# Third mixer's compact inverse: the stream step between the two products of a level moved behind the second product

## The reference

```
h   = rms_norm(x)
z   = h @ w_in                       # columns for four mixers, and four sets of merge gates
o_i = mixer_i(z_i), i = 1..4         # HGRN2, RWKV-7, GLA, mLSTM; 4 heads each
mix = sum_i (o_i @ w_branch_i) * sigmoid(z_gate_i)
x   = x + mix @ w_out
x   = x + relu(rms_norm(x) @ w_up)^2 @ w_down
y   = rms_norm(x)
```

## Time and profile before

| | us |
|---|---|
| median of 3 runs | 2150.78 |
| lowest, highest | 2146.99, 2151.19 |
| the profiled execution, its own time | 2154.51 |
| its span | 2152.6 |
| PE busy | 2074.8 |
| PEld busy | 1961.0 |
| DVE busy | 1032.9 |
| ACT busy | 607.4 |
| POOL busy | 455.1 |
| first L1336 of tile 0, last L1345 of tile 7 start at | 865.0, 1091.7 |

### The profile page before, as it was taken

How to read it: one execution, slowest core, us unless ns; L and a number is a source line. 1 busy time by engine, 2 the same in 40 slices (tenths; PEclk the granted TensorE clock), 3 DMA queues, 4 the chain that set the end, 5 groups by cost and what they waited for, 6 DMA issues and landing times.

```text
span 2152.6 us, 37101 instructions
## 1 busy us (share of the span) xinstructions
PE 2074.8 (96%) x15253; PEld 1961.0 (91%) x15253; DVE 1032.9 (48%) x1611; ACT 607.4 (28%) x821; POOL 455.1 (21%) x463
## 2 busy tenths in 40 slices
PE   6999999999999989999899999999999999999997
PEld 4998888999999879788789999999999999999996
DVE  4052334365755536444443785522222236556666
ACT  4432224332322154222222430101101023333343
POOL 1122113344554421100002671200000010000020
PEclk9999999999999999999999999999999999999999
DMA  4123225322122242111023652311112242111112
GB/s 170 41 60 85 60 81 153 101 70 65 56 72 66 84 141 85 48 42 42 23 61 142 241 190 80 128 39 49 49 39 69 79 186 90 43 49 39 49 40 100
DMA packets 50852, 177.96 MB, mean 83 GB/s; under 512 B 6481, under 2 KB 10033, under 8 KB 50497
## 3 DMA queue, kind: packets, MB, share of 16 engines
q1 hardware_dynamic: 25296, 85.77, 13.7%
q0 software_dynamic: 17648, 61.31, 8.4%
q10 hardware_dynamic: 7808, 29.41, 3.5%
HBM read 128.95 MB, written 47.51 MB: 82 GB/s over the span
## 4 chain that ended last, share of the span: by engine, by line
PE 84%; DVE 7%; issue 3%; DMA 3%; ACT 2%; POOL 0%; DVEq 0%; SPq 0%; ACTq 0%; POOLq 0%
PE PS L477 29%; PE PS L649 22%; PE PS L1567 16%; PE PS L1174 2%; DMA RING<-in_w_br 2%; PE PS L1539 1%; DMA RING<-in_w_all 1%; PE PS L1186 1%; PE PS L1035 1%; DVE CF_parts L623 1%; PE PS L1209 1%; PE PS L1202 1%; DVE AR L2596 1%; PE PS L1294 1%; PE PS L1255 0%
## 5 line engine op out<-in xcount | busy, mean ns | idle before, releaser
L477 PE MATMUL PS<-HT_parts,WHIA_parts 128*128 128x352 f32 (+1 forms) x1440 | 513.6, 357 | 9.4 <-POOL RING_parts L472 3.6
L477 PE MATMUL PS<-HT_parts,RING_parts 128*128 128x352 f32 (+1 forms) x1440 | 473.8, 329 | 1.2 <-issue 1.2
L477 PE MATMUL PS<-OT_parts,WHIA_parts 128*128 128x352 f32 (+1 forms) x1440 | 474.4, 329 | 0.0
L472 POOL TENSOR_TENSOR RING_parts<-RING,WHIA_parts 128x1024 fp32r<-128x1024 f32 x60 | 162.0, 2700 | 710.0 <-ACT WHIA_parts L467 710.0
L477 PEld LDWEIGHTS PS<-HT_parts,WHIA_parts 128*128 128x128 f32 x1440 | 277.0, 192 | 26.0 <-issue 12.2
L477 PEld LDWEIGHTS PS<-OT_parts,WHIA_parts 128*128 128x128 f32 x1440 | 277.4, 193 | 3.7 <-issue 0.3
L477 PEld LDWEIGHTS PS<-HT_parts,RING_parts 128*128 128x128 f32 x1440 | 276.7, 192 | 2.1 <-issue 2.1
L1567 PE MATMUL PS<-MIXHI_parts,CF_parts 128*128 128x352 f32 x786 | 253.8, 327 | 5.0 <-DVEq L2846 3.0
L649 PE MATMUL PS<-HT_parts,CF_parts 128*128 128x352 f32 x768 | 249.4, 325 | 0.9 <-ACT AR L616 0.9
L649 PE MATMUL PS<-HT_parts,RING_parts 128*128 128x352 f32 x768 | 249.5, 325 | 0.0
L649 PE MATMUL PS<-OT_parts,CF_parts 128*128 128x352 f32 x768 | 249.2, 325 | 0.0
(11 more groups left out here) (450 smaller groups left out, 3360.5 us busy)
## 6 DMA issues: line engine op xcount, KB each, us to landing
RING<-in_w_all SPq DMA_DIRECT2D x132, 512.0 KB, 3.7
AR<-gates POOLq DMA_DIRECT2D x32, 528.0 KB, 4.0
proj<-AR ACTq DMA_DIRECT2D x18, 537.0 KB, 5.2
AR<-proj POOLq DMA_DIRECT2D x18, 537.0 KB, 7.9
gates<-CF ACTq DMA_DIRECT2D x16, 528.0 KB, 5.3
gates<-AR ACTq DMA_DIRECT2D x16, 528.0 KB, 5.7
AR<-in_xT SPq DMA_DIRECT2D x8, 537.0 KB, 8.6
AR<-in_xT POOLq DMA_DIRECT2D x8, 528.0 KB, 6.3
```

The lines of the kernel that those rows point to most:

```text
L472: e.tensor_tensor(RING_R[:, u], RING[:, u], WHIA_R[:, u].bitcast(F32), ALU.subtract).then_inc(S(f"split{u}"), 1)
L477: last = e.matmul(out, a_[:, u, k, :], b_[:, k, t], start=first and i == 0, stop=end and i == 2)
```

## The change

It takes the one step between the two products of a level away and puts two steps behind the second product where one stood. This holds for all four levels and all eight full tiles. Every tile still has 24 steps in the same order, and no instruction is added or taken away. DVE, ACT, POOL and SP have the same programs.

```diff
                     last.then_inc(S("rw_m"), 1)
-                    steps(gate, 1)
                     e.wait_ge(S("rw_m1"), n * 6 + l)
                     e.wait_ge(S("rw_t"), t0 + rw_ti(l - 1))
                     e.sem_inc(S("select_turn"), 1)
...
                     last.then_inc(S("rw_n"), 1)
-                    steps(gate, 1)
+                    steps(gate, 2)
                     if l == 1 and not first:
                         back_to_rows(n - 1, P)
```

## The result

The change makes the kernel slower: 2193.02 us as a median of 4 executions (2175.55 to 2204.4) against 2150.99 of the kernel before (2146.99 to 2158.86), ratio 1.0181 with a 95% interval of 1.014 to 1.0222, all of it above 1. The direction was forecast; the size, +42.0 us between the medians, is nearly six times the forecast +7.2, and outside the range. All ratios with intervals here are taken over the executions within 1.5% of a kernel's fastest, so they are not the quotients of the medians (1.0195 in this case). Two later calls with 6 executions each of the changed kernel gave 1.0124 (1.008 to 1.0167) and 1.0112 (1.0049 to 1.0174). The executions of the changed kernel lie far apart, 2165 to 2204, where 75 of the kernel before lay between 2142 and 2170.

A forecast was written before the change was run, and what follows sets the result against it. PE, busy 96% of the span, was taken to bound the kernel. Seven tiles' 5.9 us, tile 0's 1.11 and three tiles' 0.5 gave +7.5, less 0.3: +7.2 on 2150.78, forecast 2158.0 us, range 2154.5 to 2161.

The forecast's parts named there:

- The sum: Changes of PE's time over four levels and eight tiles: +7.5 us, less 0.3 for DVE's earlier copy, +7.2 us.
- The clock falls in the levels: Rival: PE's idling in the levels lowers the granted clock; 31 us if in each tile, 2189; chance 0.08.
- The price of a fall: At a lower clock, 24 stream matmuls cost 0.16 us more each: 3.9 us per tile.
- In two tiles only, 2166: Milder case of the clock rival: the granted clock falls in two tiles, total time 2166 us.
- The step between the products was a full cover: In each level the step hides the wait for ACT's copy; removal gains 0.18 us, PE idles 0.50.
- second products later than 0.95 us: Sign of being wrong: second product starting over 0.95 us behind the first, meaning a dearer signal.
- Level 2's wait for DVE filled: Behind level 2 the added step fills L1336's 0.46 us wait for L2582 in seven tiles: -0.15 us each.
- Level 4 hidden: Ahead of L1387, in five tiles waiting there for DVE, PE's 0.31 us of extra work costs 0.
- the stall for "issue" halved: Behind level 4, three tiles' 0.4 us stall may stay or vanish: middle of 0 and +0.31 taken, 0.16 each.
- the rival on late code: PE's new waits let code arrive in time, removing 11.1 us of issue stalls at tile beginnings: 2145.2; chance 0.07.
- The port rival: DVE's four copies ahead of L472 all run before POOL gets in; tile 1's wait goes: 2152.6; chance 0.11.
- the deduction in the sum: Behind level 4 DVE's first L2596 may start before L472, ending its chain up to 0.2 us earlier: -0.3 us.

The follow-up runs named there:

- e0: The changed kernel run again unaltered, 6 executions in a later call: 2172.32 us, ratio 1.0124 to the kernel before.
- e1: Changed kernel plus matmuls nobody reads between the two products of every level, where PE waits: 2158.75 us, ratio 1.0026 to the kernel before.
- e6: Kernel before with steps moved from tile beginnings and ends to behind level 2's second product and ahead of L1387: 2148.90 us, ratio 0.9970.
- e10: The kernel before with steps moved into PE's waits, same kernel as e6, in another call: 2147.39 us, ratio 0.9956.
- e4: Changed kernel plus matmuls nobody reads between the products of levels 1, 2 and 4 only: 2153.37 us, ratio 0.9996 to the kernel before.

## Why the prediction was right or wrong

- **The step that failed: the clock.** The sum has no term for it; the rival "The clock falls in the levels" had it, with a chance of 0.08. Its mechanism, place and sign were there; its chance and its price were not. The prediction took a stretch of 3 us with 1.28 us idle that kept its clock as protection. The runs showed in its place that levels with 0.54, 0.54, 0.89 and 0.54 us of waits, 2.5 us within 10 where the kernel before had 0.46, lost the clock in 2 and 4 of 8 tiles in two executions and in none in a third. The stretch of rows 8 was read rightly (with its neighbours it even holds 2.6 us of waits), but one case that held said little about another.
- **The price of a fall** was put at the 24 matmuls of the levels' own steps, 3.9 us per tile. The fall comes at the end of the levels and lasts 17.1 us, 8 us per tile. "In two tiles only, 2166" should have read about 2174; the execution with two falls took 2175.55.
- **"Slower" was right for a minor reason.** The forecast called it by the waits, which the experiments put between 0 and 5.9 us; the medians moved by 42, 19 and 32 us in the three calls. That the waits and the clock point the same way is luck.
- **The step between the products was a full cover: right.** All 32 second products wait for ACT now. They start 0.88 us after the first in tiles 0 and 1 (0.87 forecast), but 0.98 in tiles 2 to 7: behind ACT's end at 0.74 PE takes 0.14 us to go on in the two tiles written out and 0.24 in the looped ones. Level 3 measured 1.24 and 1.33 (1.24 forecast). Some 2.4 us in all were missing here; the prediction had named second products later than 0.95 us as a sign of being wrong.
- **Level 2's wait for DVE filled: right.** L1336's wait is gone. The distance from the second product of level 3 to the next first product is 1.53 us, 1.54 forecast.
- **Level 4 hidden: right; the stall for "issue" halved: too dear.** In the tiles at full clock that run in the loop (2, 3, 6 and 7) L1386 stands 6.15 to 6.23 us behind the first product of level 4 (6.24 forecast), and PE waits there no longer. The stall at L477 went altogether (1.2 to 0), and the waits for "issue" at L1311 and L1317 fell from 9.9 to 6.7 us in the profiled execution. So part of the rival on late code did happen there; in e0 they are 10.4 us, so these waits change from one execution to the next.
- **The sum of the waits, +7.2: of the right size in the levels, less in the whole.** From the first product of level 1 to that of level 4 the tiles grew by 0.89 us (tile 0), 0.78 (tile 1) and 1.04 to 1.08 (each looped one), 8.0 in all, where levels 1 to 3 had 7.0 in the sum. Behind that, level 4 gave some back. At equal clock 4 us at most are left, and e1 measures +5.9.
- **The rule against the change was weighed and put aside.** TensorE: Matmul & The Clock Gate, A second HAM failure mode, of the Trainium skill says that micro-idles between groups of matmuls make the clock swing. The runs agree with it, with gaps under 1 us and 8 us per fall.
- **The port rival: did not happen, the deduction in the sum did.** In tiles 0 and 1 DVE's first copy got in ahead of L472. The first took 0.22 us, but the second lasted until L472 was done; tile 0:

```profile
876.16 2.52 DVE L2595 COPY AR<-AR 32x128 f32<-32x128 f32 x2
876.18 2.41 POOL L472 TENSOR_TENSOR RING_parts<-RING,WHIA_parts 128x1024 fp32r<-128x1024 f32 x1 [22.31 <-ACT WHIA_parts L467]
```

In the looped tiles L472 starts first, by 0.02 to 0.09 us. The wait at L1386 in tile 1 is still 1.7 us, and the fall of the clock behind it is still there.

## What to carry to other kernels

Work that covers a short wait of PE for another engine does two things: it hides the wait, and it keeps PE active. Before taking it out, list the gaps that the change leaves one behind another, not only the longest, and price a fall of the clock by how long the clock took to come back in the traces at hand. One stretch that kept its clock is no proof that another will. Where gaps exist, steps moved into them from denser places gained 6 to 8 us here (e6, e10), and even matmuls that nobody reads gained back most of the loss (e1, e4). Profile an execution more than once: three of one program differed here by 25 us.

## What the runs showed of the hardware that was not expected

- Behind gaps of 0.54, 0.54, 0.89 and 0.54 us within 10 us the granted clock fell in 0, 2 and 4 of 8 tiles of three executions of the same program. Afterwards it stayed at 0.50 for 17.1 us with PE without a wait. Behind gaps of 0.99 and 1.60 us within 5 us it did not fall (before, tile 4).
- Matmuls of 128 x 160 columns without any use (e4, 96 of them in the full tiles) made the changed kernel 0.9996 of the kernel before, from a kernel that is 1.011 to 1.018 of it.
- PE goes on 0.24 us behind the end of ACT's copy in the tiles inside a loop, and 0.14 in the two written out ahead of it. The loop alone does not explain it: behind DVE's L2582 PE went on after 0.14 us in a looped tile too.
- A DVE copy that started 0.02 us ahead of POOL's L472 took 0.22 us; the one behind it was held for 2.28 us, until L472 was done (after, tile 0).
